# Even heads invert by VectorE block transposes up to block size 32; odd heads update the retention state in two halves between the residual additions

## The reference, cut to what matters

```python
a_mat = jnp.eye(c) + jnp.einsum('bnhid,bnhjd->bnhij', kb, kc) * decay * strict
u_base = lax.linalg.triangular_solve(a_mat, vb, left_side=True, lower=True, unit_diagonal=True)
```

```python
r = r * cdec + jnp.einsum('bhck,bhcv->bhkv', k_ * kdec, v_)
...
y = (jax.nn.silu(gate) * o).astype(h.dtype) @ w_out
```

## Time and profile before

| | us |
|---|---|
| median of 3 runs | 1951.57 |
| lowest, highest | 1949.85, 1953.59 |
| the profiled execution, its time | 1950.33 |
| its span, first to last instruction | 1948.0 |
| mean granted clock | 0.979 |

### The profile page before, as it was taken

One profiled execution on the slowest core, in us unless ns is written; L12 is line 12 of the kernel. 1 busy time (PEld: TensorE's weight loads), 2 busy tenths in 40 slices (PEclk: granted clock), 3 DMA queues, 4 the chain that ended last, 5 costly groups with the idle time before them and its releaser, 6 DMA issues.

```text
span 1948.0 us, 33891 instructions
## 1 busy us (share of the span) xinstructions
PE 1849.7 (95%) x13431; PEld 1774.0 (91%) x13431; DVE 592.0 (30%) x873; ACT 617.8 (32%) x830; POOL 858.3 (44%) x1061
## 2 busy tenths in 40 slices
PE   6899998998899999999899999999997999999997
PEld 5898888987799999999899999999986999999996
DVE  2636354444310111000452344245335111111002
ACT  3625243342322222112433243333334222222112
POOL 2534435353544545446543443343334445444443
PEclk9999999998999999999999999999997999999998
DMA  5112121211222222222331432243231222222321
GB/s 146 44 34 77 38 71 43 74 37 34 59 86 80 82 86 75 86 82 81 96 112 43 136 114 87 70 125 114 61 109 57 76 86 75 86 80 77 89 81 57
DMA packets 254283, 153.22 MB, mean 79 GB/s; under 512 B 5136, under 2 KB 246549, under 8 KB 254240
## 3 DMA queue, kind: packets, MB, share of 16 engines
q1 hardware_dynamic: 239582, 139.85, 25.0%
q10 hardware_dynamic: 14658, 12.79, 2.1%
HBM read 138.26 MB, written 14.36 MB: 78 GB/s over the span
## 4 chain that ended last, share of the span: by engine, by line
PE 65%; issue 15%; POOL 9%; DVE 6%; ACT 3%; DMA 1%; DVEq 0%; POOLq 0%; ACTq 0%; SPq 0%
PE acc L456 48%; POOL w_lo L448 8%; PE acc L476 7%; PE mx L1465 6%; DVE n_xf L578 1%; PE mx L848 1%; PE mx L519 1%; DVE ca L1238 1%; POOL kdm L944 1%; DMA x_in<-in_x_sample 0%; PE acc L1620 0%; ACT L527 0%; DVE qT L1287 0%; POOL xn_lo L562 0%; ACT std L1057 0%
## 5 line engine op out<-in xcount | busy, mean ns | idle before, releaser
L448 POOL TENSOR_TENSOR w_lo<-raw,w_hi 128x256 fp32r<-128x256 f32 x932 | 709.8, 793 | 969.8 <-ACT w_hi L440 969.8
L456 PE MATMUL acc<-xn_hi,w_hi 128*128 128x288 f32 x2224 | 497.4, 305 | 3.5 <-POOL w_lo L448 1.6
L456 PE MATMUL acc<-xn_hi,w_lo 128*128 128x288 f32 x2224 | 477.2, 296 | 0.0
L456 PE MATMUL acc<-xn_lo,w_hi 128*128 128x288 f32 x2224 | 476.4, 296 | 0.0
L440 ACT ACTIVATE w_hi<-raw 128x1024 fp32r<-128x1024 f32 (+1 forms) x237 | 246.7, 1042 | 519.8 <-PE acc L456 478.3
L456 PEld LDWEIGHTS acc<-xn_hi,w_hi 128*128 128x128 f32 x2224 | 358.1, 190 | 19.2 <-issue 12.4
L456 PEld LDWEIGHTS acc<-xn_hi,w_lo 128*128 128x128 f32 x2224 | 358.9, 189 | 0.0
L456 PEld LDWEIGHTS acc<-xn_lo,w_hi 128*128 128x128 f32 x2224 | 358.6, 189 | 0.0
L592 DVE TENSOR_TENSOR x<-acc,x 128x576 f32<-128x576 f32 (+1 forms) x112 | 84.8, 757 | 318.6 <-PE acc L456 316.8
L684 DVE TENSOR_TENSOR f_h<-acc,f_g 128x576 f32<-128x576 f32 x44 | 33.3, 757 | 439.3 <-PE acc L456 439.3
L456 PE MATMUL acc<-h_hi,w_hi 128*128 128x288 f32 x704 | 151.1, 295 | 0.0
(11 more groups left out here) (321 smaller groups left out, 2203.2 us busy)
## 6 DMA issues: line engine op xcount, KB each, us to landing
raw<-in_odd_w_in SPq DMA_DIRECT2D x48, 512.0 KB, 4.0
raw<-in_ffn_w_gate SPq DMA_DIRECT2D x44, 512.0 KB, 3.7
raw<-in_ffn_w_up SPq DMA_DIRECT2D x44, 512.0 KB, 3.7
raw<-in_ffn_w_down SPq DMA_DIRECT2D x32, 512.0 KB, 3.7
raw<-in_even_w_in SPq DMA_DIRECT2D x29, 512.0 KB, 3.9
r_s<-in_state_ret SPq DMA_DIRECT2D x8, 1024.0 KB, 6.4
raw<-in_odd_w_out SPq DMA_DIRECT2D x16, 512.0 KB, 3.7
out<-r_s ACTq DMA_DIRECT2D x8, 1024.0 KB, 6.0
```

What stands on the lines that cost most here:

```text
L448: ins = nc.gpsimd.tensor_tensor(w_lo[:, d, piece], raw[:, s, piece], w_hi[:, d, piece].bitcast(F32), ALU.subtract)
L456: ins = nc.tensor.matmul(out, w, mv[:, tokens], start=first and n == 0, stop=last and n == 2)
```

## The change

In the even heads levels 2 to 16 no longer multiply into bank 3. After zi has been updated, VectorE transposes its 32 x 32 blocks into xi; up to level 16 all that is not zero lies in 32 x 32 blocks on the diagonal. Level 32 still multiplies. level_p now waits for step z, level_q for step x. In the odd heads the state update is made of two halves of 128 x 1024: rs0 before the first residual addition, rs1 before the third. The six rotary steps follow additions 2 to 7 instead of 0 to 5. The waits of ScalarE and SyncE on rs become waits on rs1.

```diff
-            o_dve.wait(act, h, "rs")
+            o_dve.wait(act, h, "rs1")
...
             o_pe.wait(dve, h, "kvs")
-            step(nc.vector.scalar_tensor_tensor(out=r_s[:, :, :].rearrange("p b n -> p (b n)"),
-                                                in0=r_s[:, :, :].rearrange("p b n -> p (b n)"), scalar=cdec_s,
-                                                in1=mx[:, :, :].rearrange("p a n -> p (a n)"), op0=ALU.mult,
-                                                op1=ALU.add), "rs")
             for m in range(KT):
+                if m in (0, 2):
+                    half = slice(m // 2 * NB // 2, (m // 2 + 1) * NB // 2)
+                    old = r_s[:, half, :].rearrange("p b n -> p (b n)")
+                    step(nc.vector.scalar_tensor_tensor(out=old, in0=old, scalar=cdec_s,
+                                                        in1=mx[:, m:m + 2, :].rearrange("p a n -> p (a n)"),
+                                                        op0=ALU.mult, op1=ALU.add), f"rs{m // 2}")
                 add_to_x(dve, phase, i, PLAIN[phase] + m, m)
-                if m < 6 and not last:
-                    if m % 3 == 0:
-                        emptied(dve, phase, i, 4 + m // 3)
-                    turn_step(dve, h + 1, m)
+                if m >= 2 and not last:
+                    n = m - 2
+                    if n % 3 == 0:
+                        emptied(dve, phase, i, 4 + n // 3)
+                    turn_step(dve, h + 1, n)
...
                 if not last:
-                    o_dve.wait(sp, h, "rs")
+                    o_dve.wait(sp, h, "rs1")
                     head_decays(h + 1)
...
                     nc.vector.tensor_tensor(zi[0:TS, TP:T], zi[0:TS, TP:T], mx[0:TS, 1, TS:2 * TS], ALU.subtract)
-                    nc.vector.tensor_tensor(xi[0:TS, TP:T], xi[0:TS, TP:T], mx[0:TS, 1, 2 * TS:3 * TS], ALU.subtract)
                 e_dve.done(nc.vector.tensor_tensor(zi[:, 0:TP], zi[:, 0:TP], mx[:, 2, :], ALU.subtract), f"z{s}")
-                if s < MASKS[-1]:
+                if s <= SQUARE // 2:
+                    e_dve.wait(dve, h, f"z{s}")
+                    if s <= 2:
+                        nc.vector.transpose(xi[0:TS, TP:T], zi[0:TS, TP:T])
+                    e_dve.done(nc.vector.transpose(xi[:, 0:TP], zi[:, 0:TP]), f"x{s}")
+                elif s < MASKS[-1]:
                     e_dve.done(nc.vector.tensor_tensor(xi[:, 0:TP], xi[:, 0:TP], mx[:, 3, :], ALU.subtract), f"x{s}")
...
-                e_dve.wait(pe, h, f"x{s // 2}")
+                e_dve.wait(pe, h, f"z{s // 2}")
                 ins = by_chunk(0, lambda c: bm[:, b, c * P:(c + 1) * P], lambda c: at(zi, c))
...
                 e_act.wait(pe, h, f"p{s}")
+                e_dve.wait(pe, h, f"x{s // 2}")
                 if s == 2:
                     e_dve.wait(pe, h, "vb")
                 ins = by_chunk(2, lambda c: at(xi, c), lambda c: at(pp, c))
-                if s < MASKS[-1]:
+                if SQUARE // 2 < s < MASKS[-1]:
                     ins = by_chunk(3, lambda c: at(pp, c), lambda c: at(xi, c))
                 if s <= 4:
-                    mm(mx[0:TS, 1, TS:2 * TS], xi[0:TS, TP:T], pp[0:TS, TP:T])
-                    ins = mm(mx[0:TS, 1, 2 * TS:3 * TS], pp[0:TS, TP:T], xi[0:TS, TP:T])
+                    ins = mm(mx[0:TS, 1, TS:2 * TS], xi[0:TS, TP:T], pp[0:TS, TP:T])
```

More of the change, by code:

```diff
@@ L161 @@
 MASKS = (1, 2, 4, 8, 16, 32, 64)
+SQUARE = 32
 SPREAD = P // 4
@@ L225 @@
 O_DVE = ("qg", "att", "r0", "r1", "r2", "r3", "of_p", "of_s", "o_both", "cen", "sq_both",
-         "on0", "y0", "on1", "y1", "yl0", "yl1", "rs")
+         "on0", "y0", "on1", "y1", "yl0", "yl1", "rs0", "rs1")
 ROTARY = ("tk", "rk", "tq", "rq")
```

## The result

The changed kernel takes 1985.62 us (1982.71 to 1987.77), the kernel before beside it 1952.58; the ratio is 1.016, with a 95% interval of 1.0142 to 1.0179. The change costs 33 us where 28 were forecast, and 1985.6 lies inside 1964 to 1991. The profiled execution took 1984.24 us, its span is 1982.3, its mean granted clock 0.967 against 0.979.

The account below looks back on a forecast made before the run. PE was taken as the bound, with a chain without slack from rs to PE ending odd heads. 1950.3 - 16.1 (even heads) + 35.7 (queues) + 9.1 (clock) = 1979.0, so 1980 with the 1.2 us profile offset; range 1964 to 1991.

Parts of the forecast that it names:

- Even heads: Fewer PE instructions in the doubling levels and sample block, and an earlier level_p(2): -16.1 us, between -13 and -17.
- The product term: Even heads: four levels lose 8 PE instructions each, 0.83 us per level, 13.3 us saved over four heads.
- the sample block: Even heads: it loses 2 instructions at two levels, 16 in all, saving 0.9 us (0 to 1.8).
- the wait of level_p on x: Even heads: level_p(2) waits for z1 in place of x1, so 1.9 us in all goes.
- The transposes: Even heads, VectorE: 0.68 us each, covered by PE work; cost 0, at most 0.25 us per head, 1 us in all.
- Odd heads on VectorE: Splitting the state update gives VectorE nothing; moved rotary steps cost nothing, 0.3 us per head at most.
- The queues: Odd heads: rs1 ends 5.35 us later, delaying unit 0 and PE; 5.1 us per head, +35.7 us (33 to 37.5).
- The clock: Odd heads: PE's standing brings one 3.2 us stretch at 1.2 GHz per head, costing 1.3 us each, +9.1 us.
- A: Odd heads: PE waits for unit 0 but the clock stays at 2.4 GHz; 1971 us, chance 0.20.
- B: From rs1 to unit 0: SyncE's wait does not reach PE, under 2.3 us lost per head; 1948 or 1935, chance 0.07.
- C: Two low-clock stretches per head, or transposes showing behind level 16; 1989 to 1995 us, chance 0.07.
- the main case: Odd heads: PE stalls before unit 0, with one slow clock stretch per head; 1980 us, chance 0.66.

Follow-up runs that it names:

- experiment 2: The changed kernel, with SyncE issuing unit 0 of the next head before its wait on rs1: 1934.10 us, ratio 0.9895 to the kernel before.
- experiment 8: The kernel with only the even heads' change, plus two more unread 128 x 512 transposes per level: 1935.83 us, ratio 0.9901.
- the kernel with the dead products: The kernel with only the even heads' change, with bank 3's products at levels 2 to 16 put back unread: 1947.10 us, ratio 0.9968.
- experiment 5: The changed kernel plus 32 unread matmuls of 288 columns after PE's last block of an odd head: 1971.10 us, ratio 1.0073.
- experiment 4: The changed kernel, with ScalarE splitting unit 0 ahead of its wait on rs1 and the two state stores: 1963.16 us, ratio 1.0048.

## Why the prediction was right, and where it was off

**What bounds the kernel: right.** Both readings, PE without gaps in the levels and a chain at the end of the odd heads without slack, are borne out; experiment 2 shows that the second alone makes the loss.

**Even heads, -16.1 forecast: probably 3 us too small.** The even part alone gave -19.5; the end of its interval, -23 to -16, touches the forecast. By the trace it was -17.7, and -19 by the head at equal clock. The product term was right as far as can be told: 13.3 forecast, 13.6 measured. What is over must be in the two others, 2.8 forecast for the wait and the sample block together: the kernel with the dead products keeps just these two and gained 6 us (4 to 9). The mis-sized term is most likely the wait of level_p on x, taken at its 1.9 us in the trace: exchanging the waits gave about 5 us, with an interval that reaches down to 2, and 1.5 us in the head at equal clock, where the recorded wait is 0.7. Where the rest comes from was not settled. The prediction has no term for the clock in the even heads; the changed kernel has heads of 104.7 us at a mean of 0.94 and of 99.6 and 100.6 at 0.98.

**The transposes, 0: right, on a thinner cover than counted.** 0.70 us each against the 0.68 taken, and no wait of PE on xi. But z32 starts 6.81 us after z16 (experiment 8) where it took 232.96 - 227.03 = 5.93, so it comes 0.9 us later and not the 0.1 to 0.2 counted; 0.7 of it is the copy into out_a, 1.06 us in place of 0.37. z16 and that copy in the kernel before:

```profile
227.03 0.69 DVE L1317 TENSOR_TENSOR zi<-zi,mx 128x512 f32<-128x512 f32 x1 [4.63 <-PE mx L1465]
...
230.10 0.37 DVE L1334 COPY out_a<-bufa 128x2 f32 x1
```

PE waits for z32 in three heads, 0.17 to 0.18 us each, where it did not before; the other 0.8 of zi's 1.3 us was there before. The Trainium skill, Vector Engine (DVE) Microarchitecture Reference, section 3.8, gave an estimate of 0.53 us by one element per cycle and lane. The trace agrees with the rate: a transpose of 64 x 64 took 0.24 us and one of 128 x 512 0.70, so 1.03 ns per column and about 0.17 us that the estimate lacks.

**Odd heads on VectorE, no gain from the split: right.** The halves take 1.28 us against 1.25, the first addition came when PE released it, and with the load out of the way (experiment 2) the rotary steps two places back cost nothing that can be told.

**The queues, 5.1 us per head and +35.7: right.** The update ends 5.3 us later (5.35 forecast), the landing is 7.2 (7.3), PE waits 5.4, in all 37.8. That PE stands the full delay holds because the chain had no slack before.

**The clock, 1.3 us per head and +9.1: this term was too small.** The step was "one such stretch per head", sized by a stretch of 3.2 us at the low level. Here 5.4 us of work ran at 1.2 GHz. With pairs 0.48 us apart in place of 0.27 that is 5.4 x (1 - 0.27 / 0.48) = 2.4 us in the head shown, and 2.0 on the mean by experiment 5: 14 us in place of 9. The odd part came out 7 us larger than forecast and the even part 2 to 3 larger, which offset each other in part; that the sum is only 5.6 us low owes something to luck.

**The rivals.** A (the clock stays up) is what experiment 5 had to build by hand; its 1971 is what that kernel measured, to the microsecond by luck, since its even part is larger and its wait longer than A's sum has them. B needed a head to lose under 2.3 us; it lost 7.35. The landing did not quicken, because the stores moved with the load, as argued; experiment 4 shows that apart from them it does, and the change would still lose. C priced two slow stretches; what came was one that was longer: 6.8 us at 1.2 GHz in five heads, of which 1.4 fell into the stall in the head shown. So C was nearer to what the clock did than the main case, and its price of 9 us more was too high: the clock's term was 5 us more.

## What to carry to other kernels

A wait placed in an in-order DMA queue holds back everything behind it, related or not: before a producer is moved later, list the issues behind each wait on it and follow each to its first user, and put loads that don't depend on the producer ahead of the wait. A chain that ends at the same moment as the bounding engine's own work shows next to no wait (0.1 us per head here) and turns every microsecond of delay into one of stall. Price a new stall of TensorE with its clock: here the clock added 2.0 us to a wait of 5.3.

## What the runs showed that I had not expected

- The low clock outlasts the stall by different times: about 3.5 us of work after 3.16 us of standing, but 5.4 us after 5.42. And two stalls of 2.90 and 2.85 us in one run left it once at 2.4 GHz and once at 1.2. With rs1 before the second addition four stalls of 3.14 or 3.15 us lowered it and a fifth of 3.14, at 1359.6, did not. The length of a gap alone did not tell; what does was not settled.
- The period of a head splits for that reason. With ScalarE's split ahead of the stores the last five periods were 69.60, 71.05, 71.09, 69.68 and 71.33 us, where the products that keep PE at work gave 72.1 in all five.
- VectorE's copies of a few columns into bufa and out_a took 0.16 to 1.06 us in the changed kernel. The slow ones end beside the ends of GpSimd instructions (220.65 + 1.06 = 221.71, and a mask of GpSimd ends at 220.41 + 1.27 = 221.68; 219.16 + 0.62 = 219.78, and a part of a low part ends at 219.75), so I take them as held by GpSimd's work; that was not tried by itself.
